# Gate rows by broadcast DMA, and the sample state laid out by sample, head and key quarter for VectorE, in a one-core decoder layer

## The chip, the core and the metric

The kernel runs on one core of a Trainium2 chip, as one program. The metric is the device time of one execution in microseconds. The core has a matrix engine (TensorE, PE in the rows), VectorE (DVE), ScalarE (ACT), GpSimd (POOL), and SyncE (SP), which here only issues DMAs. TensorE writes to PSUM; the other data live in SBUF (on chip, 128 partitions) and in DRAM.

## What is computed

One inference step of a decoder layer for a prompt of 1024 tokens and 8 single-token samples (1032 columns in all), model width 1024, everything float32. Cut to what matters here:

```
p = x @ w_in                      # pool input u | q | k | v | o | i gate, f gate (4 heads of 128)
y_pool = causal means over 2/4/8/16 tokens, minus token, per-group 128x128 map
b = cumsum(log f); m_t = running max; Dw = exp(b_t - b_s + i_s - m_t), causal
iw = exp(b + m_prev - m_t)        # weight of the carried state
s = (q k^T) * Dw
h = (s v + iw * q C) / max(|s 1 + iw * q n|, exp(-m_t))
C_new = g * C + sum_s w_s k_s v_s^T ;  n_new = g * n + sum_s w_s k_s
x1 = LN(alpha*x + [y_pool, sigmoid(o)*h] @ w_out);  x2 = LN(alpha*x1 + relu(x1 w1 + b1)^2 w2 + b2)
```

The prompt starts from a zero state. Each of the 8 samples has a state C of its own for each of the 4 heads: 32 matrices of 128 keys by 128 values, 2 MB, that are read (iw * q C), updated (one k v^T each) and returned.

## The kernel before

Activations lie transposed: channels on partitions, the 1032 tokens in the free dimension, in three blocks of 344 columns (BLK). Each float32 operand of a large product is split into a high part and a rounding rest (`x_hi`, `x_lo`, `w_hi`, `w_lo`), and a product is three float32r matmuls for each of the 8 slices of the inner dimension: 24 matmuls of 344 columns, called one product below. The order on each engine is written out by hand; counting semaphores tie the engines together.

**Projection.** Units u = 1 to 10 hold 256 weight columns each and give six products (i = 0 to 5). ScalarE evacuates each (`evac`), ScalarE and VectorE split the next weights (`split_hi`, `split_lo`). A product's bank is one of three, so it waits for the evacuation of the product three before it. Units 9 and 10 give the pool channels; VectorE forms their moving sums in `window(g, ..)`, twice a unit, after i = 3 and i = 5.

**Attention in the gaps.** The prompt is handled in 16 pairs p (4 heads, each 4 pairs of 128-token chunks). From unit 3 on one part of a pair stands behind each product (`gap_pair`): `att1`, `att2`, `att3`, so units 9 and 10 hold pairs 12, 13 and 14, 15. In att1 TensorE transposes the last pair's `h_nat`, spreads two gate rows of the head (the exponent row and iw) over 128 partitions by four matmuls of 256 columns with a 0/1 matrix (`select` by `rows_hi`, `rows_lo`), forms q k^T and transposes k and v. ScalarE (`decay_and_v`) turns the spread row into `decay` and copies v; GpSimd masks it; VectorE forms `q_inter` (q times the spread iw), `k_weighted`, `probs`, and gates the last pair's h. att2 is the state sum on TensorE and its addition to `state_ring` on VectorE, att3 numerator and denominator. att2 waits for `k_weighted`, att3 for the first `state_ring` update.

**Samples.** `sample_C` holds keys on partitions. GpSimd loads it in four DMAs after head 2. In att3 of pairs 12 to 15 TensorE multiplies one head's eight matrices with one column of q each (8 matmuls of one column). The update is in the output product.

**Output product.** Units 11 to 22: for each block four units of two products. After each product of the first block from the second on, TensorE makes an outer product of 512 columns (`outer`), four states at a time, from k (`kv_sample_nat`) and v masked by VectorE (`v_masked`, `vmask`); VectorE adds it to four matrices (`new_C`). The eighth stands behind the first product of unit 15. Then come the transposes of the mixed rows (`mix_T`), which wait for all of `C_new` in the case of the first tile, and the first layer norm (`ln1_a`). GpSimd stores the state (`C_s`) and only then loads `x_nat`, which `ln1_a` needs. The feed-forward part behind it is not touched.

## Time and profile before

| | us |
|---|---|
| median of 3 runs | 1136.58 |
| lowest, highest | 1135.8, 1137.31 |
| the profiled execution | 1137.68 |
| its span in the trace | 1134.8 |
| TensorE busy in the span | 1097.5 |

Start times below are microseconds from the start of the span. Between start times of neighbours in a TensorE timeline lies the true pace; a matmul's own length there contains its pipeline and overlaps the next. Lines L1666 and L1670 are the helpers for a matmul and a transpose, so groups are told apart by the names of the tiles (output<-inputs). A float32 matmul has two records.

### The profile page before, as it was taken

What the parts mean: (1) busy time and instruction counts of PE and PEld (TensorE: products, weight loads), DVE (VectorE), ACT (ScalarE), POOL (GpSimd) and SP (SyncE); (2) the same over time, 40 slices, a digit from 0 to 9 for tenths busy, and PEclk for the clock granted to TensorE, in tenths of its full rate; (3) what the DMA queues carried; (4) which work ended last, traced back from release to release, by engine and by line L of the source; (5) the groups of instructions that cost most, each with busy time, mean ns of one, the idle gap of its engine ahead of it and who ended that gap; (6) DMA issues with size and microseconds to landing.
All of it is one profiled execution on the core that took longest, in us unless ns stands there. A gap on an engine that the chain in (4) does not pass through costs nothing. (4 is left out here: it accounts for less than half of the span.)

```text
span 1134.8 us, 19572 instructions
## 1 busy us (share of the span) xinstructions
PE 1097.5 (97%) x8192; PEld 1078.6 (95%) x8192; DVE 663.8 (58%) x926; ACT 489.5 (43%) x694; POOL 90.3 (8%) x110
## 2 busy tenths in 40 slices
PE   7999999999999999999999999999999999999993
PEld 5999999999978899999999999999999999999993
DVE  5522222224567566495555655557766677878876
ACT  5622424241254366665554554545453323334022
POOL 4000000010010122000000000000000000000056
PEclk9999999999999999999999999999999999999997
DMA  9211111122115553124436354468734425334212
GB/s 252 75 47 33 40 39 39 41 84 62 38 45 164 185 175 106 51 66 156 151 121 184 113 151 147 131 183 271 271 103 141 146 80 168 115 114 165 75 49 101
DMA packets 93073, 132.70 MB, mean 117 GB/s; under 512 B 5369, under 2 KB 54105, under 8 KB 92996
## 3 DMA queue, kind: packets, MB, share of 16 engines
q1 hardware_dynamic: 89452, 121.13, 33.7%
q0 software_dynamic: 3552, 10.59, 3.2%
q8 instruction: 51, 0.84, 0.3%
q14 instruction: 18, 0.15, 0.0%
HBM read 97.04 MB, written 34.89 MB: 116 GB/s over the span
## 5 line engine op out<-in xcount | busy, mean ns | idle before, releaser
L1666 PE MATMUL bank<-x_hi,w_hi 128*128 128x344 f32 (+1 forms) x792 | 261.7, 330 | 3.0 <-DVE x_lo L1231 1.4
L1666 PE MATMUL bank<-x_hi,w_lo 128*128 128x344 f32 (+1 forms) x792 | 254.4, 321 | 0.0
L1666 PE MATMUL bank<-x_lo,w_hi 128*128 128x344 f32 (+1 forms) x792 | 254.1, 321 | 0.0
L1666 PE MATMUL bank<-x_hi,d_lo 128*128 128x258 f32 x1000 | 231.3, 282 | 0.0
L1666 PEld LDWEIGHTS bank<-x_hi,d_lo 128*128 128x128 f32 x1000 | 171.7, 189 | 0.0
L1666 PEld LDWEIGHTS bank<-x_hi,w_hi 128*128 128x128 f32 (+1 forms) x792 | 148.4, 187 | 10.8 <-issue 3.8
L1666 PEld LDWEIGHTS bank<-x_hi,w_lo 128*128 128x128 f32 (+1 forms) x792 | 148.1, 187 | 1.3
L1666 PEld LDWEIGHTS bank<-x_lo,w_hi 128*128 128x128 f32 (+1 forms) x792 | 148.2, 187 | 1.1
L1666 PE MATMUL bank<-x_hi,s_hi 128*128 128x258 f32 x448 | 126.5, 282 | 1.8 <-DVE s_raw_lo L1359 1.8
L1666 PE MATMUL bank<-x_lo,s_hi 128*128 128x258 f32 x448 | 126.5, 282 | 0.0
L1666 PE MATMUL bank<-t_hi,s_hi 128*128 128x258 f32 x336 | 95.2, 283 | 0.0
L1666 PE MATMUL bank<-t_lo,s_hi 128*128 128x258 f32 x336 | 95.1, 283 | 0.0
L1666 PEld LDWEIGHTS bank<-x_hi,s_hi 128*128 128x128 f32 x448 | 84.7, 189 | 2.0 <-DVE s_raw_lo L1359 2.0
L1666 PEld LDWEIGHTS bank<-x_lo,s_hi 128*128 128x128 f32 x448 | 84.5, 189 | 0.0
L1666 PE MATMUL bank<-x_hi 128*128 128x258 f32 x288 | 81.6, 283 | 0.0
L1666 PE MATMUL bank<-x_hi,x_lo 128*128 128x258 f32 x280 | 79.3, 283 | 2.3 <-DVE y_acc L1493 2.3
L1666 PE MATMUL bank<-x_lo,x_hi 128*128 128x258 f32 x288 | 81.4, 283 | 0.0
L1012 DVE TENSOR_TENSOR w_lo<-w_raw,w_hi 128x2048 fp32r<-128x2048 f32 x23 | 53.0, 2302 | 46.3 <-ACT w_hi L646 45.8
L903 ACT ACTIVATE x_hi<-x_lo_raw 128x2064 fp32r<-128x2064 f32 (+1 forms) x28 | 48.0, 1714 | 73.5 <-DMA x_lo_raw<-h_ops 73.5
L1666 PE MATMUL bank<-x_lo,d_lo 128*128 128x258 f32 x248 | 70.0, 282 | 0.0
L1666 PE MATMUL bank<-x_lo 128*128 128x258 f32 x248 | 69.9, 282 | 0.0
L1666 PEld LDWEIGHTS bank<-t_lo,s_hi 128*128 128x128 f32 x336 | 63.7, 189 | 0.0
(311 smaller groups left out, 2262.6 us busy)
## 6 DMA issues: line engine op xcount, KB each, us to landing
h_ops<-h_unit SPq DMA_DIRECT2D x56, 258.0 KB, 2.5
x_lo_raw<-h_ops SPq DMA_DIRECT2D x14, 1032.0 KB, 5.2
s_raw<-in_w_ff SPq DMA_DIRECT2D x14, 1024.0 KB, 7.0
w_raw<-in_w_out SPq DMA_DIRECT2D x12, 1024.0 KB, 5.1
x_lo_raw<-h_ops SPq DMA_DIRECT2D x14, 774.0 KB, 4.6
d_raw<-in_w_ff SPq DMA_DIRECT2D x9, 1024.0 KB, 7.4
w_raw<-in_w_in SPq DMA_DIRECT2D x16, 512.0 KB, 5.3
h_ops<-t_out SPq DMA_DIRECT2D x28, 258.0 KB, 5.1
```

The lines of the kernel that those rows point to most:

```text
L903: A(h_slot(t, XH), h_slot(t, XLS), ACT.Copy).then_inc(dh_hi, 1)
L1012: V.tensor_tensor(WL[:, q, :], RAW[:, q, :], WH[:, q, :].bitcast(F32), ALU.subtract).then_inc(lo_done, 1)
L1666: return nc.tensor.matmul(out, lhsT, rhs, start=start, stop=stop, skip_group_check=True)
```

## The change

**Gate rows.** The `select` matmuls, their high and low rows and their preparation on GpSimd, VectorE and ScalarE are gone. GpSimd writes the two rows of all heads to DRAM in two DMAs; SyncE reads them back in eight steps of two DMAs (`load_rows`), each giving 128 partitions the same 512 tokens (256 KB) of one head, in a ring of three; `decay` and `q_inter` read the ring in SBUF.

**Samples.** `sample_C` now has sample and head (32) times key quarter (4) on the partitions and 32 keys by 128 values in each. q, k and v of the samples are transposed in unit 9, sent to DRAM and back in nine DMAs in that layout. VectorE multiplies and adds eight keys at a time (`q_times_C`, four calls in unit 10); one small matmul adds the quarters. The update is two calls of `new_C` on VectorE alone, at the second and third unit of the output product; `outer` and `vmask` are gone. The C store stands behind the first `x_nat` loads. Core of the diff:

```diff
+        rows_d = nc.dram_tensor("gate_rows_d", (2, NH, SEQ), F32, kind="Internal").ap()
+
+        def row_slice(p, g):
+            return BR[:, p // 2 % 3, g, 2 * P * (p % 2):2 * P * (p % 2 + 1)]
...
+            def load_rows(d):
+
+                h, t0 = d // 2, 4 * P * (d % 2)
+                if d == 0:
+                    sp.wait_ge(rows_out, 32)
+                elif d >= 3:
+                    sp.wait_ge(E_ready, 4 * (d - 2))
+                    sp.wait_ge(qi_ready, 2 * (d - 2))
+                for g in range(2):
+                    sp.dma_start(BR[:, d % 3, g, :], rows_d[g, h:h + 1, t0:t0 + 4 * P].to_broadcast([P, 4 * P])).then_inc(bc_in[d % 3], 16)
...
+                if u >= 4:
+                    load_rows(u - 4)
...
+                if u == U_OUT:
+                    load_rows(7)
...
+            pool.wait_ge(dve_row, ROW_NEGM)
+            pool.dma_start(rows_d[0, :, :], TN[0:NH, pr]).then_inc(rows_out, 16)
+            pool.wait_ge(act_row, 4)
+            pool.dma_start(rows_d[1, :, :], RC[32:32 + NH, pr]).then_inc(rows_out, 16)
...
+                    if h == NH - 1 and j == 0:
+                        pool.wait_ge(kvs_read, 1)
+                        pool.dma_start(sn_d.rearrange("c r d -> r c d"), SN[0:32, :, :]).then_inc(sn_out, 16)
+                    elif h == NH - 1 and j == 1:
+                        pool.wait_ge(sn_out, 16)
+                        for q in range(4):
+                            pool.dma_start(QKS[32 * q:32 * (q + 1), :, :],
+                                           sn_d[0:2, :, 32 * q:32 * (q + 1)].rearrange("c r x -> r c x")).then_inc(qk_in, 16)
+                        for q in range(4):
+                            pool.dma_start(VS[32 * q:32 * (q + 1), :], sn_d[2]).then_inc(vs_in, 16)
...
-                    for s in range(NH):
-                        pool.dma_start(C0[:, s, :, :], a["state_C"][0, :, s, :, :].rearrange("b d e -> d b e"))\
-                            .then_inc(c_in, 16)
+                    for q in range(4):
+                        pool.dma_start(C0[32 * q:32 * (q + 1), :, :], state_v(a["state_C"], q)).then_inc(c_in, 16)
...
+                if t == 0:
+                    store_C(0)
+                    store_C(1)
...
+                    if UCH[u, f] == 0 and b == 0:
+                        act.wait_ge(qC_ready, 4)
                     A(Y[:, UCH[u, f], blk(b)], src, ACT.Copy).then_inc(gemm_read, 1)
...
-                act.wait_ge(bc_ready, p + 1)
+                act.wait_ge(bc_in[p // 2 % 3], 32 * (p // 6 + 1))
                 if p:
                     act.wait_ge(P_ready, p)
                 for i in range(2):
-                    A(E[:, i, :], B_[:, P * i:P * (i + 1)], ACT.Exp,
+                    A(E[:, i, :], row_slice(p, 0)[:, P * i:P * (i + 1)], ACT.Exp,
...
+                    if u == 9 and i == 2:
+                        act.wait_ge(kvs_T, 1)
+                        A(SN[0:32, :, :], B_[0:32, 0:384].rearrange("p (i n) -> p i n", i=3), ACT.Copy).then_inc(kvs_read, 1)
...
-            dve.wait_ge(act_row, 8)
-            V.tensor_tensor(RBL[0:NH, pr], TN[0:NH, pr], RBH[0:NH, pr].bitcast(F32), ALU.subtract)
-            row(V.tensor_tensor(RBL[32:32 + NH, :], RC[32:32 + NH, :], RBH[32:32 + NH, :].bitcast(F32),
-                                ALU.subtract), ROW_LO)
...
-                V.tensor_tensor(QI[:, :, :].rearrange("p i n -> p (i n)"), QKV[h % 2][:, 0, cs], B_[:, 256:512],
+                V.tensor_tensor(QI[:, :, :].rearrange("p i n -> p (i n)"), QKV[h % 2][:, 0, cs], row_slice(p, 1),
...
+                if p == NPAIR - 1:
+                    V.tensor_copy(ST[:, 7, :, :], N_[:, 264:296].rearrange("p (b h) -> p h b", h=NH))
...
+            def q_times_C(x):
+
+                dve.wait_ge(c_in, 64)
+                dve.wait_ge(qk_in, 64)
+                if x:
+                    dve.wait_ge(qC_ready, x)
+                step(V.tensor_tensor(PRODQ[:, :, :], C0[:, 8 * x:8 * (x + 1), :], of_planes(0, 8 * x, 8), ALU.mult))
+                for n in (4, 2):
+                    step(V.tensor_tensor(PRODQ[:, 0:n, :], PRODQ[:, 0:n, :], PRODQ[:, n:2 * n, :], ALU.add))
+                if x:
+                    step(V.tensor_tensor(PRODQ[:, 0, :], PRODQ[:, 0, :], PRODQ[:, 1, :], ALU.add))
+                    V.tensor_tensor(RP[:, :], RP[:, :], PRODQ[:, 0, :], ALU.add).then_inc(qC_ready, 1)
+                else:
+                    V.tensor_tensor(RP[:, :], PRODQ[:, 0, :], PRODQ[:, 1, :], ALU.add).then_inc(qC_ready, 1)
...
+                if u == 6:
+                    step(V.tensor_reduce(ROWSEL[:, :, :].rearrange("p b h -> p (b h)"),
+                                         IDN[:, :].rearrange("p (q r) -> p r q", q=4), AX.X, ALU.add))
+                    step(V.tensor_tensor(ST[:, 9, :, :].rearrange("p h b -> p (h b)").rearrange("p (b h) -> p b h", h=NH),
+                                         ROWSEL[:, :, :], iw_s.rearrange("p h b -> p b h"), ALU.mult))
+                    step(V.tensor_reduce(IW[:, 0:1], ST[:, 9:10, :, :].rearrange("p o h b -> p o (h b)"), AX.X, ALU.add))
...
+                    if u == 10 and i < 3:
+                        q_times_C(i)
+                        if i == 2:
+                            q_times_C(3)
...
+            def new_C(x):
+
+                dve.wait_ge(vs_in, 64)
+                if x:
+                    dve.wait_ge(C_new, x)
+                planes = C0[:, 16 * x:16 * (x + 1), :]
+                step(V.tensor_tensor(PROD[:, :, :], VS[:, :].rearrange("p (o e) -> p o e", o=1).to_broadcast([P, 16, DH]),
+                                     of_planes(1, 16 * x, 16), ALU.mult))
+                stt(planes, planes, IW[:, 0:1], PROD[:, :, :], ALU.mult, ALU.add).then_inc(C_new, 1)
+
...
                 b, j = (u - U_OUT) // 4, (u - U_OUT) % 4
-                if u == U_OUT:
-                    vmask(0)
                 if b == 0:
-                    vmask(2 * j + 1)
-                    new_C(2 * j)
                     split_lo(u + 2)
-                    if j < 3:
-                        vmask(2 * j + 2)
-                    new_C(2 * j + 1)
                     cat_lo_part(1 + j // 2, j % 2 == 0)
+                    if j in (1, 2):
+                        new_C(j - 1)
                 else:
...
-                    pe.wait_ge(qi_ready, p)
                     pe.wait_ge(kw_ready, p)
...
-                for g in range(2):
-                    mm(B_[:, 256 * g:256 * (g + 1)], SEL[:, g, h, :], RBH[:, cs], True, False)
-                    last = mm(B_[:, 256 * g:256 * (g + 1)], SEL[:, g, h, :], RBL[:, cs], False, True)
-                last.then_inc(bc_ready, 1)
...
-                if p >= NPAIR - NH:
-
-                    s = p - (NPAIR - NH)
-                    if s == 0:
-                        pe.wait_ge(c_in, 16 * NH)
-                        pe.wait_ge(prod_ready, 1)
-                        mm(N_[:, 300:364], ONES[:, :], ST[:, 0:2, :, :].rearrange("p a h b -> p (a h b)"))
-                    for b in range(NS):
-                        last = mm(N_[:, 264 + b:265 + b], C0[:, s, b, :], ST[:, 2, s, b:b + 1])
+                if p == NPAIR - NH:
+                    pe.wait_ge(prod_ready, 1)
+                    last = mm(N_[:, 300:364], ONES[:, :], ST[:, 0:2, :, :].rearrange("p a h b -> p (a h b)"))
+                elif p == NPAIR - 1:
+                    pe.wait_ge(qC_ready, 4)
+                    last = mm(N_[:, 264:296], RP[:, :], ROWSEL[:, :, :].rearrange("p b h -> p (b h)"))
...
+                    if u == 9 and i == 1:
+                        pe.wait_ge(smp_n, 1)
+                        for x, rows in enumerate((ST[:, 2, :, :], SM[:, 1, :, :], ST[:, 8, :, :])):
+                            last = tr(B_[0:32, P * x:P * (x + 1)], rows.rearrange("p x y -> p (x y)"))
+                        last.then_inc(kvs_T, 1)
...
-                    pe.wait_ge(C_new, 32)
+                    pe.wait_ge(nat_read, 2)
...
-                        else:
-                            pe.wait_ge(nat_read, 1)
-                            outer(2 * j + f - 1)
...
-                        if b == 1 and j == f == 0:
-                            outer(7)
```

TensorE, att1 of pair 14, before (`h_nat` is the last pair's output, `qkv_56` the q, k, v of the head):

```order
L1670 MATMUL bank<-identity,h_nat 128x128 x2
L1666 MATMUL bank<-rows_hi,select 128x256
L1666 MATMUL bank<-rows_lo,select 128x256
L1666 MATMUL bank<-rows_hi,select 128x256
L1666 MATMUL bank<-rows_lo,select 128x256
L1666 MATMUL bank<-qkv_56 128x128 x2
L1670 MATMUL bank<-identity,qkv_56 128x128 x4
L1666 MATMUL bank<-x_hi,w_hi 128x344
```

and now:

```order
L1724 MATMUL bank<-identity,h_nat 128x128 x2
L1720 MATMUL bank<-qkv_56 128x128 x2
L1724 MATMUL bank<-identity,qkv_56 128x128 x4
L1720 MATMUL bank<-x_hi,w_hi 128x344
L1720 MATMUL bank<-x_lo,w_hi 128x344
```

The four matmuls with `select` are gone; the transposes stand directly ahead of q k^T.

VectorE, unit 10, from pair 14's last att1 operation on, before (`state_ring` is att2's update, `small` att3's):

```order
L1106 TENSOR_TENSOR y_acc<-bank,y_acc 128x256
L1138 SCALAR_TENSOR_TENSOR state_ring<-state_ring,bc_cols,bank 128x129 x2
L1146 TENSOR_TENSOR small<-bank,gate_cols 128x2
L1148 SCALAR_TENSOR_TENSOR small<-bank,small 128x2
L1153 COPY sample_tmp<-bank 128x8
L1156 RECIPROCAL small<-small 128x2
L1113 TENSOR_TENSOR q_inter<-qkv_56,bank 128x256
```

and now (`state_prod_q` and `state_qC` belong to `q_times_C`):

```order
L1143 TENSOR_TENSOR y_acc<-bank,y_acc 128x256
L1245 TENSOR_TENSOR state_prod_q<-sample_C,state_qk 128x1024
L1247 TENSOR_TENSOR state_prod_q<-state_prod_q 128x512
L1247 TENSOR_TENSOR state_prod_q<-state_prod_q 128x256
L1252 TENSOR_TENSOR state_qC<-state_prod_q 128x128
L1175 SCALAR_TENSOR_TENSOR state_ring<-state_ring,bc_cols,bank 128x129 x2
L1245 TENSOR_TENSOR state_prod_q<-sample_C,state_qk 128x1024
L1247 TENSOR_TENSOR state_prod_q<-state_prod_q 128x512
L1247 TENSOR_TENSOR state_prod_q<-state_prod_q 128x256
L1249 TENSOR_TENSOR state_prod_q<-state_prod_q 128x128
L1250 TENSOR_TENSOR state_qC<-state_qC,state_prod_q 128x128
L1183 TENSOR_TENSOR small<-bank,gate_cols 128x2
```

Two further calls, ten rows, stand between att3 of pair 14 and `q_inter` of pair 15.

VectorE, output product, second unit of the first block, before:

```order
L1260 TENSOR_TENSOR v_masked<-kv_sample_nat,identity 32x512
L1269 SCALAR_TENSOR_TENSOR sample_C<-sample_C,bc_cols,bank 128x128 x4
L1012 TENSOR_TENSOR w_lo<-w_raw,w_hi 128x2048
L1260 TENSOR_TENSOR v_masked<-kv_sample_nat,identity 32x512
L1269 SCALAR_TENSOR_TENSOR sample_C<-sample_C,bc_cols,bank 128x128 x4
L1231 TENSOR_TENSOR x_lo<-y_acc,x_hi 128x4x344
```

and now (the last row begins the next unit):

```order
L1055 TENSOR_TENSOR w_lo<-w_raw,w_hi 128x2048
L1297 TENSOR_TENSOR x_lo<-y_acc,x_hi 128x4x344
L1324 TENSOR_TENSOR state_prod<-state_v,state_qk 128x2048
L1326 SCALAR_TENSOR_TENSOR sample_C<-sample_C,state_decay,state_prod 128x2048
L1055 TENSOR_TENSOR w_lo<-w_raw,w_hi 128x2048
```

The maskings and eight small updates of a unit have become one pair of 2048 columns, behind `x_lo`.

## Rows read from the trace of the kernel before

**Rows 1.** Page, part 1: busy time, share of span and instructions of TensorE.
```profile
PE 1097.5 (97%) x8192; PEld 1078.6 (95%) x8192; DVE 663.8 (58%) x926; ACT 489.5 (43%) x694; POOL 90.3 (8%) x110
```

**Rows 2.** TensorE timeline, att1 of pair 4: start, length, engine, instruction.
```profile
124.06 0.37 PE L1666 MATMUL bank<-rows_hi,select 128*128 128x256 f32 x1
...
124.62 0.61 PE L1666 MATMUL bank<-qkv 128*128 128x128 f32 x4
```

**Rows 3.** TensorE timeline, units 9 and 10, at pairs 13 and 14.
```profile
278.58 0.46 PE L1666 MATMUL bank<-v_aug,probs 128*128 128x129 f32 x2 [1.04 <-DVE state_ring L1138]
...
279.54 2.29 PE L1666 MATMUL bank<-sample_tmp,sample_C 128*128 128x1 f32 x16
281.70 0.63 PE L1666 MATMUL bank<-x_hi,w_hi 128*128 128x344 f32 x1
...
288.22 0.38 PE L1670 MATMUL bank<-identity,h_nat 128*128 128x128 f32 x2
...
289.71 0.41 PE L1666 MATMUL bank<-x_hi,w_hi 128*128 128x344 f32 x1
...
298.69 1.84 PE L1666 MATMUL bank<-sample_tmp,sample_C 128*128 128x1 f32 x16
300.40 0.40 PE L1666 MATMUL bank<-x_hi,w_hi 128*128 128x344 f32 x1
...
304.27 0.38 PE L1670 MATMUL bank<-identity,h_nat 128*128 128x128 f32 x2
...
316.44 1.98 PE L1666 MATMUL bank<-y_acc,w_pool_sb 128*128 128x344 f32 x6
```

**Rows 4.** Busy by window; the number before the last two is the granted clock.
```profile
282.00:284.00 2.00, 2.00 (x8) 2.00 (x8) 1.90 (x9) 1.47 (x3) 0.00 (x0) 0.50 0.00 0
372.00:376.00 4.00, 4.00 (x29) 4.00 (x28) 0.90 (x1) 0.00 (x0) 1.68 (x3) 1.00 0.98 267
```

**Rows 5.** TensorE timeline, output product, to the first mix transposes.
```profile
335.11 0.42 PE L1666 MATMUL bank<-x_hi,w_hi 128*128 128x344 f32 x1
...
340.11 0.42 PE L1666 MATMUL bank<-x_hi,w_hi 128*128 128x344 f32 x1
...
369.11 1.12 PE L1666 MATMUL bank<-v_masked,kv_sample_nat 32*128 32x512 f32 x2
371.54 0.63 PE L1670 MATMUL bank<-identity,y_acc 128*128 128x128 f32 x4 [1.31 <-DVE sample_C L1269]
...
386.30 0.42 PE L1666 MATMUL bank<-x_hi,w_hi 128*128 128x344 f32 x1 [0.62 <-DVE w_lo L1012]
```

**Rows 6.** VectorE timeline, end of unit 9 and unit 10.
```profile
281.87 0.16 DVE L1146 TENSOR_TENSOR small<-bank,gate_cols 128x2 f32<-128x2 f32 x1 [3.20 <-PE bank L1666]
...
288.08 2.28 DVE L1012 TENSOR_TENSOR w_lo<-w_raw,w_hi 128x2048 fp32r<-128x2048 f32 x1
290.28 0.41 DVE L1113 TENSOR_TENSOR q_inter<-qkv,bank 128x256 f32<-128x256 f32 x1
...
305.82 0.42 DVE L1113 TENSOR_TENSOR q_inter<-qkv,bank 128x256 f32<-128x256 f32 x1 [4.62 <-ACT decay L723]
306.46 0.42 DVE L1116 TENSOR_TENSOR k_weighted<-bank,gate_cols 128x256 f32<-128x256 f32 x1 [0.22 <-ACT v_aug L728]
...
311.87 0.73 DVE L1138 SCALAR_TENSOR_TENSOR state_ring<-state_ring,bc_cols,bank 128x129 f32<-128x129 f32 x2
```

**Rows 7.** ScalarE timeline, the evacuation ahead of pair 15's decay.
```profile
304.46 0.46 ACT L680 ACTIVATE y_acc<-bank 128x344 f32<-128x344 f32 x1 [2.60 <-PE bank L1666]
```

**Rows 8.** VectorE timeline, output product: `vmask`, then `x_lo` of a block.
```profile
338.66 0.67 DVE L1260 TENSOR_TENSOR v_masked<-kv_sample_nat,identity 32x512 f32<-32x512 f32 x1
...
341.26 1.59 DVE L1231 TENSOR_TENSOR x_lo<-y_acc,x_hi 128x1376 fp32r<-128x1376 f32 x1
```

**Rows 9.** DMA issues by line, size and time to landing: nearest broadcast load.
```profile
ln_gb<-in_ln_b POOLq DMA_DIRECT2D x1, 512.0 KB, 5.1
```

**Rows 10.** VectorE timeline, first residual of the first normalisation.
```profile
378.49 1.28 DVE L1299 SCALAR_TENSOR_TENSOR res_nat<-x_nat,bank 128x512 f32<-128x512 f32 x2 [5.59 <-DMA x_nat<-in_x_prompt]
```

More of the change, by code:

```diff
@@ L197, in build_layer @@
         pool_step, smp_kept, wsum_ready = sem("pool_step"), sem("smp_kept"), sem("wsum_ready")
-        bc_ready, s_ready, kvT_ready = sem("bc_ready"), sem("s_ready"), sem("kvT_ready")
+        s_ready, kvT_ready = sem("s_ready"), sem("kvT_ready")
+        rows_out, bc_in = sem("rows_out"), [sem(f"bc_in{x}") for x in range(3)]
         dC_ready, num_ready = sem("dC_ready"), sem("num_ready")
@@ L557, in _ @@
             G.memset(TN[0:NH, :], 1.0).then_inc(pool_step, 1)
-            pool.wait_ge(pool_step, 4)
+            pool.wait_ge(pool_step, 2)
             G.memset(TN[0:NH, pr].rearrange("h (c t) -> h c t", t=P)[:, :, 0:1], 0.0).then_inc(consts, 1)
@@ L603, in _, with store_C @@
             pool.dma_start(a["n_p"][0, 0, :, :], NN[32:36, :]).then_inc(nat_out, 16)
-            for h in range(NH):
-                pool.wait_ge(C_new, NS * (h + 1))
-                pool.dma_start(a["C_s"][0, :, h, :, :].rearrange("b d e -> d b e"), C0[:, h, :, :]).then_inc(c_out, 16)
+            def store_C(x):
+                pool.wait_ge(C_new, x + 1)
+                for q in range(4):
+                    pool.dma_start(state_v(a["C_s"], q)[:, 16 * x:16 * (x + 1), :],
+                                   C0[32 * q:32 * (q + 1), 16 * x:16 * (x + 1), :]).then_inc(c_out, 16)
             pool.wait_ge(nat_out, 16 * 7)
```

90 lines of the change are left out of this document (33 added, 57 removed).

## The prediction

> **What bounds the kernel now.** First the page's busy shares: TensorE is busy for 1097.5 us of a span of 1134.8, VectorE for little more than half [rows 1]. So an instruction taken off TensorE shortens the run by the time to the next start behind it, as long as VectorE and ScalarE deliver in time; work off the other engines brings nothing by itself. Then the TensorE timeline of the stretches that the change touches: the true cost of an inserted piece is the distance of start times, since lengths overlap. Last, the VectorE timeline of units 9 and 10, because there VectorE is already the last to arrive: TensorE stands 1.04 us ahead of pair 13's att3 until the first `state_ring` update, which queues behind a window sum [rows 3].
>
> A product with a following float32 step takes 3.87 us (300.40 to 304.27) [rows 3]; without the slower first matmul (0.40 long, the others about 0.32) 3.79. The att1 between two products takes 1.49 (288.22 to 289.71), and att2 and att3 together the rest of the 16.05 to the next att1 at 304.27, which holds three products and pair 14's sample matmuls: 1.24 [rows 3]. I call T the start of unit 10's first product, 281.70 in the trace.
>
> **Gate rows.** The four `select` matmuls take 0.56 us from their first start to that of q k^T (124.06 to 124.62) [rows 2]. There are 16 pairs: 14 stand ahead of T, which makes 7.8 us, and two behind. The operands of `decay` and `q_inter` now come by DMA. GpSimd's two writes are issued when the rows exist, before unit 3; SyncE's reads stand in its queue behind the weights of unit u and ahead of those of unit u + 1, and are issued about two units ahead of their use. A pair takes 16.05 us less the samples' 1.71, 14.3 us (288.22 to 304.27, 298.69 to 300.40) [rows 3], so two units are 57 us. The nearest row for such a load, 512 KB spread over 128 partitions, took 5.1 us to land [rows 9]; a step here moves as much. Cost zero, with 50 us of cover. The ScalarE and VectorE splits of the rows that fall away lie beside full TensorE work: zero.
>
> **Samples, ahead of T.** Eight one-column matmuls cost 1.71 us in pair 14 (298.69 to 300.40) and 2.16 in pair 13 (279.54 to 281.70) [rows 3]. Pair 12 I take as 1.7. Three transposes of 32 columns are added, two of them moved here from the output product; I take 0.1 us each, 0.3. Ahead of T: 7.8 + 1.7 + 2.2 - 0.3 = 11.4 us. Pair 13's wait stays: both sides of it move up by the same 0.56 us.
>
> **Unit 10.** Before, T to the first pool map is 34.74 us (281.70 to 316.44) [rows 3]. In it TensorE ran at half clock: the granted clock was 0.50 at 282 to 284 [rows 4], and the first product took 6.52 us instead of 3.87 (281.70 to 288.22) [rows 3]. Ahead of the fall stood the idle 1.04 us and then the one-column matmuls. The half-clock loss is 2.65 us. TensorE's own work after the change: 34.74 - 2.65 - 2 x 1.71 - 2 x 0.56 + 0.2 for the new small matmul = 27.75 us. That is the floor.
>
> But VectorE gets four `q_times_C` in this unit, which stand ahead of what TensorE waits for. Their price, from the nearest rows: a multiplication of 1024 columns a little over half of the split's 2.28 for 2048 [rows 6], 1.22; a sum of 512 as the masking in 0.67 [rows 8], of 256 as `q_inter` in 0.41, of 128 between that and the 0.16 of a two-column one [rows 6], 0.3. With about 0.03 for each wait between dependent steps that is 2.7 for the first and 3.0 for the others, 11.7 in all. The ends: 10 us if the narrow sums cost 0.16, 16 if broadcast and in-place operands cost a third more. I take 11.7, since the masking row has broadcast operands too and is no slower than its width.
>
> VectorE from T: att3 of pair 13 and the window sum, 0.17 and 6.1 (281.87 to 288.08, less a copy); the weight split 2.2 (to 290.28); att1 of pair 14, 1.4 (four of 0.41, overlapping) [rows 6]: T + 9.9. Four calls, one state update of 0.8 and att3's small steps of 0.5: T + 22.9. Now ScalarE, which has waited for the last call because the products of `q_times_C` lie in the channel that it evacuates next, needs what the trace shows from that evacuation (304.46) [rows 7] to `k_weighted` (306.46) [rows 6], 2.0 us, less the 0.24 in which `decay` waited for the spread rows: `k_weighted` starts at T + 24.7 and ends at T + 25.1. From its start to the next state update are 5.41 us (306.46 to 311.87) [rows 6], with a window sum in it; its first half ends at T + 30.5.
>
> TensorE from T: product 3.87, att1 1.49 - 0.56, product, att2 0.35 (after a wait of 0.6 for pair 14's `k_weighted`), product, att3 0.89, product, att1, product: T + 23.1, where it waits 2.0 us for pair 15's `k_weighted`. Then att2 and a product to T + 29.3, and 1.2 us for the state update; att3 and the small matmul 1.1: T + 31.6. So unit 10 gives 34.7 - 31.6 = 3.1 us instead of the 7.0 that TensorE's work alone would give. The chain is VectorE's from T on; whether the first product still runs at half clock does not matter.
>
> **The start of the output product** hangs on the pool maps and their evacuation as before, at the same distance. The last window sum ends some 2 us ahead of its map. No change.
>
> **Output product.** With an outer product a product takes 5.00 us (335.11 to 340.11) [rows 5], without one 3.79: 1.21, seven times, 8.5 us. The eighth stands ahead of the first mix transposes with 1.31 us of waiting: 369.11 to 371.54, 2.4 us [rows 5]. Two transposes gone: 0.2. VectorE's first residual waits 5.59 us for `x_nat`, which GpSimd loads behind the state stores [rows 10]; with the loads first this goes, and with it, I expect, TensorE's 0.62 us for `w_lo` at 386.30 [rows 5]. Sum 11.7 us. The new update is two operations of 2048 columns twice, 2 x 2.28 each time [rows 6], in a unit of 7.6 us in which VectorE has also 2.28 for the split and 1.59 for `x_lo` [rows 8]: 8.5 us, 0.9 more than the unit, in two units in a row. The split of unit u + 2 ends some 1.6 us or more ahead of its use, so I take zero; without that cover it costs 1 to 2 us. GpSimd's eight store DMAs now stand ahead of its first normalisation; they are issued by the time VectorE has its numbers.
>
> **Sum.** 11.4 + 3.1 + 11.7 = 26.2 us. From the profiled 1137.68 that gives 1111.5; this execution is 1.1 above the median of 1136.58, so the forecast is 1110.4.
>
> **The rivals.**
>
> A. VectorE keeps up: the calls are shorter, or ride in gaps. Then unit 10 falls to its floor, 3.9 us less: 1106.5. For it: the rows bound the narrow sums only loosely. Against: even at 10 us the chain is above the floor by 2. Chance 0.15.
>
> B. The clock. The new wait of 2.0 us and the one of 1.2 behind it could bring TensorE to 1.2 GHz again. In the trace 1.04 us of waiting followed by one-column matmuls was followed by the fall, while 1.31 us ahead of the mix transposes was not: the clock stood at 1.00 at 372 to 376 [rows 4, 5]. A product then costs 2.65 us more: 1113.1. Chance 0.18. The Trainium skill, "TensorE: Matmul & The Clock Gate", section "HAM oscillation — how this bites in real kernels", says that waits between bursts of matmuls let the clock fall and that each fall is paid anew; by it, the time would be the 1113.1 of this rival. The 1.31 us here, without a fall, does not bear that out for short waits.
>
> C. VectorE is slower than its rows, 16 us for the calls: 4.3 us later at the end of unit 10, 1114.7. Chance 0.12.
>
> D. Slower than before: the spread rows come late. ScalarE's `decay` in unit d + 3 waits for the load issued at the start of unit d + 1, and pair by pair TensorE behind it. Each of eight loads may take 57 us; what it takes beyond is paid in full, and 26.2 us are eaten at 60.3 us a load. At 61 us the time would be 1110.4 + 8 x 4 = 1142.4. The landing of 5.1 us [rows 9] and queues that idle between weight loads speak against it. Chance 0.03.
>
> **How the numbers follow.** Forecast 0.52 (1108 to 1112), A 0.15, B 0.18, C 0.12, D 0.03. The range takes in A, B and C with a microsecond beyond A's and C's ends for the terms outside unit 10: 1105.5 to 1116. About 0.2% (2.3 us) is what a measurement can tell from no change; faster by more than that 0.95, within it 0.02, slower 0.03.
>
> **What would show it.** No `select` row, and 0.93 us from `h_nat` to the next product instead of 1.49. In unit 10 a TensorE wait of about 2 us ahead of the last att2, released by `k_weighted`, and about 1 us ahead of the last att3, released by `state_ring`. Products 3.8 us apart in the first block of the output product, no wait of VectorE for `x_nat`. I am wrong if `decay` waits for a DMA, if the calls take over 4 us or under 2.4, if PEclk falls in unit 10, or if `w_lo` is late in units 13 to 16.

## The result: 20 us faster, 6 us less than forecast

| | before | after |
|---|---|---|
| median, us | 1136.19 (4 runs) | 1116.25 (4 runs, 1114.24 to 1116.7) |
| the profiled execution | 1137.68 | 1116.19 |
| its span | 1134.8 | 1114.4 |

The ratio is 0.9828, 95% interval 0.9816 to 0.984. The forecast was 1110.4 with a range of 1105.5 to 1116.0: the direction was right, the size was not, and the median lies 0.25 us above the range. Five more runs of the changed kernel beside new runs of the one before gave 1116.46 and 0.9832 (0.9818 to 0.9845).

The first thing to read is by how much the changed kernel is ahead at places that both kernels have. Each time is the start of a row in the TensorE timelines of the two profiled executions.

| place | before | after | ahead by | gained since the last | forecast |
|---|---|---|---|---|---|
| first matmul of the gates | 15.61 | 17.70 | -2.09 | -2.1 | 0 |
| first product of unit 1 | 31.38 | 34.09 | -2.71 | -0.6 | 0 |
| T, first product of unit 10 | 281.70 | 274.11 | 7.59 | 10.3 | 11.4 |
| first pool map | 316.44 | 306.03 | 10.41 | 2.8 | 3.1 |
| first product held by x_lo of the feed-forward part | 475.57 | 452.91 | 22.66 | 12.25 | 11.7 |
| first matmul of the down projection held by y_acc | 800.94 | 779.28 | 21.66 | -1.0 | 0 |
| the next one held by y_acc | 1061.86 | 1041.68 | 20.18 | -1.5 | 0 |
| span | 1134.8 | 1114.4 | 20.4 | 0.2 | 0 |

So the three stretches that the forecast worked out gave 25.4 of its 26.2 us. The other 5 went in two places to which it had given no thought: the first 34 us, and a wait about 400 us behind the last edited instruction. (The profiled times differ by 21.5 us and not by 20.4, since 1.1 us less lies outside the span in after; and the profiled execution of before is 1.5 above the median of the later runs, which is why the medians differ by 19.9.)

The page of after, part 1 (busy time, share of the span, instructions), answers to [rows 1]. TensorE's busy time fell by 24.7 us, the span by 20.4: some of what was taken off it became waiting.

```profile
PE 1072.8 (96%) x8051; PEld 1060.7 (95%) x8051; DVE 667.9 (60%) x905; ACT 486.8 (44%) x692; POOL 97.1 (9%) x122
```

**Unit 10.** The TensorE timeline of after, answering to [rows 3] (start, length, engine, instruction, in brackets the wait ahead of it and what ended it):

```profile
273.22 0.46 PE L1720 MATMUL bank<-v_aug,probs 128*128 128x129 f32 x2 [0.99 <-DVE state_ring L1175]
...
274.11 0.41 PE L1720 MATMUL bank<-x_hi,w_hi 128*128 128x344 f32 x1
...
277.97 0.38 PE L1724 MATMUL bank<-identity,h_nat 128*128 128x128 f32 x2
278.18 0.61 PE L1720 MATMUL bank<-qkv 128*128 128x128 f32 x4
...
278.98 0.40 PE L1720 MATMUL bank<-x_hi,w_hi 128*128 128x344 f32 x1
...
283.75 0.71 PE L1720 MATMUL bank<-v_aug,k_weighted 128*128 128x129 f32 x4 [0.74 <-DVE k_weighted L1153]
...
299.27 0.71 PE L1720 MATMUL bank<-v_aug,k_weighted 128*128 128x129 f32 x4 [1.47 <-DVE k_weighted L1153]
...
304.92 0.46 PE L1720 MATMUL bank<-v_aug,probs 128*128 128x129 f32 x2 [1.15 <-DVE state_ring L1175]
...
306.03 0.54 PE L1720 MATMUL bank<-y_acc,w_pool_sb 128*128 128x344 f32 x1
```

The reader sees the forecast chain: pair 13's wait is still there (0.99); att2 of pair 14 waits 0.74 (0.6 was forecast), the last att2 1.47 (2.0), the last att3 1.15 (1.2). T to the first pool map is 31.92 us; 31.6 was forecast. The first product behind T takes 3.86 us (274.11 to 277.97), where it took 6.52 at half clock before [rows 3, 4]. The att1 from `h_nat` to the next product takes 1.01 us (277.97 to 278.98), not the forecast 0.93.

VectorE's timeline of after in the same unit, the first call, the start of the second, the end of the fourth, and pair 15's first two operations, answers to [rows 6]:

```profile
284.28 1.21 DVE L1245 TENSOR_TENSOR state_prod_q<-sample_C,state_qk 128x1024 f32<-128x1024 f32 x1
...
286.71 0.29 DVE L1252 TENSOR_TENSOR state_qC<-state_prod_q 128x128 f32<-128x128 f32 x1
286.92 0.73 DVE L1175 SCALAR_TENSOR_TENSOR state_ring<-state_ring,bc_cols,bank 128x129 f32<-128x129 f32 x2
287.56 1.22 DVE L1245 TENSOR_TENSOR state_prod_q<-sample_C,state_qk 128x1024 f32<-128x1024 f32 x1
...
297.00 0.29 DVE L1250 TENSOR_TENSOR state_qC<-state_qC,state_prod_q 128x128 f32<-128x128 f32 x1
298.45 0.42 DVE L1150 TENSOR_TENSOR q_inter<-qkv,rows_bc 128x256 f32<-128x256 f32 x1 [1.16 <-ACT decay L765]
298.80 0.42 DVE L1153 TENSOR_TENSOR k_weighted<-bank,gate_cols 128x256 f32<-128x256 f32 x1
```

The first call takes 2.64 us (284.28 to 286.92), the second 2.98 (287.56 to 290.54). VectorE reached T + 10.17 with its first call; T + 9.9 was forecast. Its last call ends at T + 23.2, 0.3 later than forecast. `k_weighted` starts at T + 24.69; T + 24.7 was forecast. That this agrees to 0.01 us is luck: from ScalarE's evacuation behind the last call (297.39) to `k_weighted` (298.80) it is 1.41 us and not the 1.76 of the forecast, which made good the 0.3.

**Output product.** ScalarE's timeline of after (two evacuations in a row), then TensorE's first mix transposes, then VectorE's update of half of the state and its first residual:

```profile
323.59 0.46 ACT L828 ACTIVATE y_acc<-bank 128x344 f32<-128x344 f32 x1 [3.13 <-PE bank L1720]
...
327.36 0.46 ACT L828 ACTIVATE y_acc<-bank 128x344 f32<-128x344 f32 x1 [0.27 <-PE bank L1720]
```
```profile
349.75 1.03 PE L1724 MATMUL bank<-identity,y_acc 128*128 128x128 f32 x8
```
```profile
337.13 2.29 DVE L1324 TENSOR_TENSOR state_prod<-state_v,state_qk 128x2048 f32<-128x2048 f32 x1
339.45 2.35 DVE L1326 SCALAR_TENSOR_TENSOR sample_C<-sample_C,state_decay,state_prod 128x2048 f32<-128x2048 f32 x1
...
353.71 1.28 DVE L1358 SCALAR_TENSOR_TENSOR res_nat<-x_nat,bank 128x512 f32<-128x512 f32 x2
```

A product takes 3.77 us now (323.59 to 327.36) and took 5.00 [rows 5]. Neither the transposes nor the residual waits; 1.31 and 5.59 us of waiting are gone [rows 5, 10], and no `w_lo` is late.

**The start.** TensorE's timelines at the last x tile, before and after, each followed by GpSimd's two large constant loads of the same kernel. (These rows of before were not read for the prediction.)

```profile
14.47 1.42 PE L1670 MATMUL bank<-identity,x_nat_all 88*128 88x88 f32 x8 [1.54 <-DMA x_nat_all<-in_x_prompt]
15.61 0.57 PE L1666 MATMUL bank<-x_hi,w_hi 128*36 128x344 f32 x1
```
```profile
8.20 0.56 POOL L547 DMA_DIRECT2D state_pool_nat<-in_state_pool  x1
8.73 0.82 POOL L548 DMA_DIRECT2D w_pool_sb<-in_w_pool  x1
```
```profile
16.55 1.44 PE L1724 MATMUL bank<-identity,x_nat_all 88*128 88x88 f32 x8 [1.86 <-DMA x_nat_all<-in_x_prompt]
17.70 0.57 PE L1720 MATMUL bank<-x_hi,w_hi 128*36 128x344 f32 x1
```
```profile
5.13 0.55 POOL L572 DMA_DIRECT2D state_pool_nat<-in_state_pool  x1
5.67 0.81 POOL L573 DMA_DIRECT2D w_pool_sb<-in_w_pool  x1
```

With the `select` preparation gone from the head of GpSimd's program, its constant loads go out 3.07 us earlier, and the x tile on which the gates wait lands 2.08 us later. SyncE's queue issues the x tiles, GpSimd's the constants: 496 KB, of which TensorE first reads at 31 us in before, now fall among tiles that it waits for. The clock made it worse: windows of after, then of before (the number before the last two is the granted clock, of which 1.00 is 2.4 GHz and 0.50 is 1.2):

```profile
18.00:20.00 2.00, 2.00 (x8) 1.27 (x7) 0.98 (x2) 0.46 (x1) 0.00 (x0) 0.50 1.10 260
```
```profile
18.00:20.00 2.00, 2.00 (x14) 1.43 (x13) 0.00 (x0) 0.00 (x0) 0.00 (x0) 1.00 1.09 250
```

The gates of before began at half clock too, but from their first matmul to unit 1 it is 15.77 us there and 16.39 in after (17.70 to 34.09): 0.6 us more.

**The down projection.** The first matmul that waits for `y_acc`, before and then after, with the window behind it in after:

```profile
800.94 0.36 PE L1666 MATMUL bank<-x_hi,x_lo 128*128 128x258 f32 x1 [2.28 <-DVE y_acc L1493]
```
```profile
779.28 0.55 PE L1720 MATMUL bank<-x_hi,x_lo 128*128 128x258 f32 x1 [3.48 <-DVE y_acc L1547]
```
```profile
779.00:781.00 2.00, 1.72 (x8) 1.75 (x9) 2.00 (x2) 2.00 (x2) 0.00 (x0) 0.55 1.06 387
```

It waits 1.2 us longer, and then TensorE runs at half clock (0.55 in this window, 1.00 at the same place before), which costs 1.5 more. Nothing in this stage was changed.

The wait hangs on one load. SyncE's queue in before, after, and e7_rows (the kernel before with the gate rows alone, below): a weight load, the last stores of `h_ops` (a DRAM tensor for the hidden activations), and the load of `h_ops`, which waits until they have landed.

```profile
782.07 0.45 SPq L437 DMA_DIRECT2D d_raw<-in_w_ff  x1
...
783.18 0.43 SPq L412 DMA_DIRECT2D h_ops<-t_out  x1
790.55 0.92 SPq L443 DMA_DIRECT2D x_lo_raw<-h_ops  x2
```
```profile
759.21 1.22 SPq L469 DMA_DIRECT2D d_raw<-in_w_ff  x1
...
761.02 0.43 SPq L444 DMA_DIRECT2D h_ops<-t_out  x1
768.76 0.92 SPq L475 DMA_DIRECT2D x_lo_raw<-h_ops  x2
```
```profile
771.51 0.46 SPq L456 DMA_DIRECT2D d_raw<-in_w_ff  x1
...
772.63 0.43 SPq L431 DMA_DIRECT2D h_ops<-t_out  x1
781.43 0.92 SPq L462 DMA_DIRECT2D x_lo_raw<-h_ops  x2
```

Measured back from the end of TensorE's preceding matmuls (798.66, 775.80 and 788.15), the load is issued 8.11, 7.04 and 6.72 us ahead. In all sixteen profiled executions this lead and TensorE's wait add up to 10.3 to 10.6 us: each microsecond by which the load goes out later is one of waiting.

### The profile page after: what moved, and what is told of

Its sections match the earlier page's. It is cut to its first block and busy times, and to the rows that moved or that the text cites. A ratio compares the mean times of both kernels' runs of the same rounds, so it can differ in the third digit from the quotient of the medians.

```text
span 1114.4 us, 19275 instructions
## 1 busy us (share of the span) xinstructions
PE 1072.8 (96%) x8051; PEld 1060.7 (95%) x8051; DVE 667.9 (60%) x905; ACT 486.8 (44%) x692; POOL 97.1 (9%) x122
```

## The experiments

Each kernel ran five or more times beside the kernel before. A difference between a variant and the changed kernel is one of medians, with the changed kernel at 1116.46 in the first group. The intervals of the ratios are 1.0 to 2.3 us to either side, so such a difference is good to 1 or 2 us. A shorter time is one between places in a profiled execution: in after and e0_after, the one kernel that was profiled twice, stretches of this kind agreed to some 0.1 us where the clock did the same.

**The changed kernel again (e0_after).**

> The changed kernel again, unaltered. Theory S (the start is late because GpSimd's constant loads now go out 3.1 us earlier and share the DMA engines with the x tiles): the first gate matmul again near 17.7 us of the trace (15.6 in the kernel before), ratio to before 0.982 to 0.984. Rival N (the late start in the one profile was scatter of that execution): the first gate matmul falls back towards 15.6 and the profile's span is 2.7 us shorter. The wait ahead of the first matmul of the down projection (3.48 us after, 2.28 before) is also looked at: if it is scatter of the DMA, it differs here.

1116.46 us, the first gate matmul at 17.59, the wait at the down projection 3.52 us with half clock behind it. Both losses came back: neither is scatter of one execution.

**GpSimd's work put back (e1_prep).**

```diff
+            G.memset(sel, 0.0).then_inc(pool_step, 1)
+            G.affine_select(out=sel, in_=sel, ...).then_inc(pool_step, 1)
+            G.tensor_copy(sel, sel).then_inc(pool_step, 1)
             G.memset(VA[:, :, DH:DH + 1], 1.0).then_inc(consts, 1)
             ...
             pool.dma_start(CN[r:r + n, :], ...)
```

> The changed kernel with GpSimd's three 1024-column operations (3.1 us) put back ahead of its constant loads; their output is not used. Theory S: the constant loads go out at 4.9 us again, the first gate matmul starts near 15.6, unit 1 near 31.4, and the time falls by 2.7 us against the changed kernel, to about 1113.5. Rival N: no difference, 1116.2. Rival V (the late start comes from VectorE's removed memsets or something else at the start, not from the loads): the gate matmul stays at 17.7.

1111.5 us, ratio 0.9789 (0.9773 to 0.9805): 5.0 us less than the changed kernel, for three operations more. TensorE's timeline and the window at 16 us:

```profile
14.75 0.83 PE L1731 MATMUL bank<-identity,x_nat_all 88*128 88x88 f32 x8 [1.04 <-DMA x_nat_all<-in_x_prompt]
15.37 0.37 PE L1727 MATMUL bank<-x_hi,w_hi 128*36 128x344 f32 x1
```
```profile
16.00:18.00 2.00, 2.00 (x15) 1.40 (x14) 0.77 (x2) 0.13 (x1) 0.00 (x0) 1.00 1.06 317
```

The gates start 2.33 us earlier and run at 1.00, so that unit 1 starts at 30.08, 4.0 us ahead of after's 34.09. The theory named the cause rightly and was short by the clock: it had reckoned with that of the kernel before. The rivals (scatter; VectorE's removed memsets) are out. The clock's part is not the loads' alone. e7_rows, whose GpSimd does the same as that of the kernel before up to its constant loads, has full clock too and takes 14.69 us from the first gate matmul to unit 1, as e1_prep does with 14.71, where before takes 15.77.

**The same order put into the kernel before (e5_early).** Only the preparation moved behind the constant loads, which go out at 1.83 us there:

> The kernel before with nothing changed but GpSimd's select preparation, which stands behind its constant loads instead of ahead of them, so that these go out 3.1 us earlier. Theory S: the first gate matmul moves from 15.6 to about 17.7, unit 1 from 31.4 to 34.1, and the kernel is 2.7 us slower than before, ratio 1.0024. Rivals N and V: no difference, ratio 1.000.

1138.9 us, ratio 1.0029 (1.0017 to 1.0041).

```profile
17.84 0.57 PE L1666 MATMUL bank<-x_hi,w_hi 128*36 128x344 f32 x1
```

The gates start 2.23 us later than in the kernel before, unit 1 at 33.68 instead of 31.38. The order of loads is a cost of its own, in a kernel that has none of the change. (The clock column of this execution stands at 1.00 in the window 18 to 20 us, though a gate matmul lasts 0.49 us there, as at 0.50 in after, and 0.32 at full clock. In the first microseconds the length of the matmuls is the safer sign.)

**The two large constant loads late (e2_late).**

```diff
+            pool.wait_ge(x_in[5], 16)
             pool.dma_start(SPN[0:NS * NBUF, :], ...)
             pool.dma_start(WP[:, :, :], ...)
```

> The changed kernel with the two large constant loads (state_pool_nat 240 KB, w_pool_sb 256 KB) issued only when the sixth x tile has landed. Theory S: 496 KB less between the x tiles at some 250 GB/s are 2.0 us, so the first gate matmul starts 2 us before that of the changed kernel or earlier, 15.0 to 15.7, and the time is 2 to 3.5 us shorter than the changed kernel's, 1112.7 to 1114.2. Rival N: no difference. Rival L (the loads are then late for the two transposes ahead of unit 1 at 31 to 34 us): a wait for a DMA there, no gain.

1111.27 us, ratio 0.9788 (0.9773 to 0.9802), 5.2 us less than the changed kernel. The gates start at 14.82, no wait for a DMA stands between them and unit 1 (29.55), so rival L is out. The forecast 15.0 to 15.7 was a little too late; the rest of the gain is again clock, which was at half from about 11 to 14 us, beside the transposes, and not beside the gates.

The Trainium skill, "DMA: Bandwidth & Descriptors", section "Queues, rings and completion order", says that each DMA engine goes round between the queues for which it has work, a packet at a time. By that rule a load in another queue is served beside the x tiles however late it is wanted, and e1, e2 and e5 agree with it.

**The gate rows alone (e7_rows).** The kernel before with the rows by DMA, and with the three GpSimd operations kept:

> The kernel before with only the gate rows by DMA; GpSimd's three operations ahead of its constant loads are kept, the samples are untouched. Theory: each att1 is 0.48 us shorter (the trace of after has 1.01 us from the transposes of h_nat to the next product instead of 1.49), 16 pairs give 7.7 us, ratio 0.9932 or 1128.5. The prediction's own price of 0.56 would give 9.0 us, ratio 0.9921. Rival: the row loads or the added waits cost something, and less than 7 us are left.

1129.97 us, ratio 0.9944 (0.9929 to 0.9958): 6.0 us, less than either 7.7 or 9.0. From pair to pair, `h_nat` of att1 comes 0.47 us earlier each time (1.86 us ahead of before at pair 1, 7.10 at pair 12: 5.24 in eleven pairs, 0.476 each). That is the theory's price. In the profiled execution, 1.35 us faster than the median, the clock added to it, 1.1 us at the start and 1.1 at unit 10's first product. But at the down projection there is the longer wait, with half clock behind it, as in after:

```profile
791.69 0.36 PE L1680 MATMUL bank<-x_hi,x_lo 128*128 128x258 f32 x1 [3.54 <-DVE y_acc L1507]
```

So the samples' part of the change is not needed for a long wait there. But it is not shown that the gate rows make it in both kernels, for the load of `h_ops` is late in two ways. Here the last store is issued on time, 15.5 us ahead of the matmuls' end as in before, and 8.8 us pass until the load; in the four kernels without row loads it is 7.0 to 7.4. In the eleven profiled executions with the whole change or a variant of it the issue of the weight load ahead of the last stores lasts 1.2 to 1.8 us instead of 0.45, the last store is issued 0.7 to 1.3 us later for it, and the distance from it to the load is 6.7 to 7.9. Why that issue lasts longer is not known.

The row loads themselves cost the projection nothing: in after the 16 took 5.4 us to land in the median (5.1 was forecast), and no `decay` waited for one.

**Unit 10 without the calls (e3_nocalls).**

> The changed kernel with the multiplications of q and C in unit 10 left out: each of the four calls is one small operation (0.3 and three of 0.15 us), so the sample outputs are not those of the reference. The theory (unit 10 is VectorE's chain): the waits ahead of the last att2 and att3 go, T to the first pool map falls from 31.9 to the floor of 27.8 us, 1112.1. Rival W (the window sums alone hold the last state update): a wait of 1 us or more stays ahead of the last att3 and 1113.5 or more is measured.

1112.71 us, ratio 0.9793 (0.9781 to 0.9806). The last att2 and att3 no longer wait. T is at 274.56, the first pool map at

```profile
303.36 0.54 PE L1715 MATMUL bank<-y_acc,w_pool_sb 128*128 128x344 f32 x1
```

which makes 28.80 us; 27.8 was expected. So the calls cost 3.1 us in unit 10 (31.92 - 28.80). The floor of the prediction, 27.75, was about 1 us too low: 0.74 of it is the wait ahead of pair 14's att2, which stands here too, and which VectorE's window sum and weight split cause ahead of the first call; 0.16 is the price of the spread rows, taken too high twice. This kernel leaves out what the calls compute; the next one keeps it.

**Two calls later (e4_later).**

```diff
-                    if u == 10 and i < 3:
+                    if u == 10 and i < 2:
                         q_times_C(i)
-                        if i == 2:
-                            q_times_C(3)
...
             split_lo(U_OUT + 1)
+            q_times_C(2)
+            q_times_C(3)
```

`state_qC`'s matmul goes behind the fourth product of the output product, the samples' numerator behind it, and ScalarE's `wait_ge(qC_ready, 4)` is gone, since `state_prod_q` lies elsewhere.

> The changed kernel with two of the four q_times_C calls and the sample numerator moved behind the weight split of the first output-product unit, where VectorE idled 6.4 and 3.7 us in the trace; state_prod_q lies in a free slot of the ring of gate rows, so ScalarE's evacuation no longer waits for the calls. Theory: as without the calls, T to the first pool map 27.8 to 28.2 us, no loss later, 1112.2. Rival M (moved, not removed): the calls come back as a wait of TensorE for w_lo or x_lo in the output product, and at most 1 us is gained.

1113.23 us, ratio 0.9799 (0.9786 to 0.9811). TensorE's last att2, last att3 and first pool map, none with a wait:

```profile
297.36 0.60 PE L1727 MATMUL bank<-v_aug,k_weighted 128*128 128x129 f32 x4
...
301.58 0.38 PE L1727 MATMUL bank<-v_aug,probs 128*128 128x129 f32 x2
...
302.47 0.45 PE L1727 MATMUL bank<-y_acc,w_pool_sb 128*128 128x344 f32 x1
```

From T (273.83) that is 28.64 us, as low as without the calls. From the pool map to the next common place, the first `x_lo` wait of the feed-forward part, it is 147.03 us, and 146.88 in after: the moved calls (from 315.78 on) came back nowhere, and rival M is out. Of the 3.28 us, some were lost to the clock later in this execution: behind a wait of 1.75 us, which after has too and where its clock held, it fell:

```profile
466.60 0.39 PE L1727 MATMUL bank<-x_hi,s_hi 128*128 128x258 f32 x1 [1.75 <-DVE s_raw_lo L1420]
```
```profile
467.00:471.00 4.00, 4.00 (x23) 4.00 (x23) 3.15 (x3) 2.02 (x2) 0.00 (x0) 0.60 1.01 305
```

**Both together (e6_both).**

> The later calls and the late constant loads together. The two stretches lie apart, so the gains should add: 4.0 and 2 to 3.5 us off the changed kernel, 1108.7 to 1110.2. Rival: one gain is given back at a later wait (the first of the down projection, whose length hangs on DMA landings), 1111 or more.

1110.23 us, ratio 0.9765 (0.9752 to 0.9777): with h2_best below the fastest kernel of the study, 6.2 us below the changed one. The two gains of 5.2 and 3.2 add to 8.4 and gave 6.2, a difference hardly larger than the 1 to 2 us that such a sum is good to. In its profile unit 1 starts at 29.79 and the pool maps at 298.45, 7.58 us ahead of after, nearly the sum; then the clock falls behind the 1.75 us wait (462 to 467 us, as in e4_later), which takes 1.5. So something was given back, as the rival said, but not where it said: the wait at the down projection is 3.46 us, as in after.

**What lengthens the wait at the down projection: addresses or the queue? (g1_addr, g2_poolq, h1_bothq)** Two things of the change reach that far: two new DRAM tensors move `h_ops` by 80 KB (in e7_rows one of them, by 32 KB), and SyncE's queue, which loads and stores for the down projection, has 16 transfers more behind it.

> The changed kernel with its two new DRAM tensors declared behind h_first and h_ops, so that these lie at the addresses that they have in the kernel before. Every kernel run so far with the row loads waits 3.1 to 3.6 us ahead of the first matmul of the down projection that needs y_acc, with TensorE at half clock behind it; both without them wait 1.8 and 2.3 us and keep the clock. Theory Q (the shifted DRAM addresses of h_ops slow its stores and loads): the wait falls to about 2.3, the clock stays at 1.00, 2.5 us are gained, 1113.8. Rival P (the 16 row loads in SyncE's queue change how its later transfers fall): no difference, wait 3.1 to 3.6, 1116.3.

> The changed kernel with the 16 row loads issued by GpSimd instead of SyncE, so that SyncE's queue is that of the kernel before; the DRAM tensors stay where the changed kernel has them. Theory P: the wait ahead of the down projection's matmul falls to about 2.3 us and the clock stays, 1113.8. Theory Q: no difference, 1116.3. Rival G (GpSimd's issues delay its masking of decay): waits of TensorE ahead of att3 in units 4 to 8, slower than 1116.3.

1115.13 us (0.9833, 0.9813 to 0.9853) and 1115.84 us (0.9835, 0.9814 to 0.9856). The waits were 2.86 and 2.90 us, the clock fell behind both. Each seemed to give half of the wait; in time neither gave anything that can be told, for the kernel before was faster in this group too (1134.45), and the ratios are that of the changed kernel, 0.9832.

> The changed kernel with both edits together: new DRAM tensors declared last, and the row loads issued by GpSimd. Each alone left a wait of 2.9 us ahead of the down projection where the changed kernel has 3.5 and the kernel before 2.3. If both contribute (theories P and Q each half), the wait is 2.3 here and the clock stays at 1.00 behind it, 1113.5. If neither matters (rival R: something else that the kernels with row loads share), 2.9 to 3.5 again and 1115.5 to 1116.3.

1115.77 us (0.9822, 0.9806 to 0.9839), a wait of 2.76 us with half clock behind it. The two do not add up, so neither is shown to be a cause.

**Each of them in the kernel before (h3_pad, h4_loads).**

> The kernel before with an 80 KB DRAM tensor declared ahead of h_first and h_ops (one row of it is written once), so that their addresses are those of the changed kernel. Theory Q: the wait ahead of the down projection rises from 2.3 to 2.9 or 3.5 us and TensorE is at half clock behind it, 1137.5 to 1138.5. Otherwise the wait stays at 1.8 to 2.3, ratio 1.000.

> The kernel before with 16 loads of the same shape and size as the row loads (one row of 512 words to 128 partitions) in SyncE's queue at units 4 to 8, into a tile that is free then; nothing reads them. Theory P: the wait ahead of the down projection rises to 2.9 to 3.5 us, half clock behind it, 1137.5 to 1138.5. Otherwise it stays at 1.8 to 2.3 and the time at that of the kernel before. It shows too what the loads cost the projection itself: nothing by the prediction.

1135.45 us (1.0002, 0.9993 to 1.0011) and 1135.73 us (1.0001, 0.9992 to 1.001). The rows at the down projection, h3_pad and then h4_loads:

```profile
801.25 0.36 PE L1670 MATMUL bank<-x_hi,x_lo 128*128 128x258 f32 x1 [1.90 <-DVE y_acc L1497]
```
```profile
801.08 0.36 PE L1676 MATMUL bank<-x_hi,x_lo 128*128 128x258 f32 x1 [1.86 <-DVE y_acc L1503]
```

Neither lengthens the wait, nor the issue of the weight load (0.45 and 0.46 us). Theories P and Q are both out as sole causes. h4_loads shows too, by a clean comparison, that 16 broadcast loads of 256 KB cost the projection nothing.

**Everything together (h2_best).**

> Two of the four calls later, the two large constant loads late, DRAM tensors last, row loads by GpSimd. The sum of what each brought: 1110.2 with the first two, and 0 to 2.7 us more from the other two, 1107.5 to 1110.2. Rival: an added fall of the clock at a wait of 1 to 2 us gives it back, 1110 or more.

1110.38 us (0.9775, 0.976 to 0.979), like e6_both: the wait was 3.58 us again.

## Why the prediction fell short, step by step

**"The four `select` matmuls take 0.56 us from their first start to that of q k^T": the mis-sized term.** It was priced by the distance that they span [rows 2]. But with them gone the q k^T starts 0.21 us behind the `h_nat` transposes (277.97 to 278.18 in after), where the first `select` matmul had started 0.13 behind (288.22 [rows 3] to 288.35). TensorE's timeline of before:

```profile
288.35 0.37 PE L1666 MATMUL bank<-rows_hi,select 128*128 128x256 f32 x1
```

The att1 shrank from 1.49 to 1.01: 0.48. Over 14 pairs 6.65 us instead of 7.8, a shortfall of 1.2. The distance to take was that of the neighbours on both sides of the piece, less what they will then keep between them.

**The samples ahead of T, 3.6 us: right.** What is left of the gain there is 7.59 + 2.71 - 6.65 = 3.65.

**"The ScalarE and VectorE splits ... lie beside full TensorE work: zero", and no word on GpSimd's: the missing step.** The account of the change names the preparation on GpSimd as gone; the prediction did not ask what stands behind it in GpSimd's program, and so put the whole start at nothing. It is the constant loads, and they came 3.07 us forward into the one stretch of the kernel where TensorE waits for DMA. It cost 2.1 us in DMA and 0.6 in clock against the kernel before; e1_prep and e2_late show that 4.0 and 4.5 us can be had there up to unit 1, since the clock can also stay up. Without these 2.7 us the median would have lain inside the range. A step taken out moves every instruction behind it, and that can be a loss.

**Unit 10, 31.6 us: right, 31.92.** Its chain held place by place, and so did the price of the calls (four calls of 2.6 to 3.2 us; 11.7 forecast in all). The wait at the last att2 was 1.5 and not 2.0 us, pair 14's att2 0.74 and not 0.6. The floor behind it, 27.75, was too low by 0.9 to 1.0: a wait that the prediction had itself put into the chain was left out of the floor. The value of rival A was thus 3.1 to 3.3 and not 3.9 us.

**Rival B, the clock in unit 10: did not come.** The waits of 1.47 and 1.15 us were followed by no fall; the window 282 to 290 and those behind it stand at 1.00. But clock falls did take part elsewhere, at places where only the length or the time of a wait changed. The prediction's "whether the first product still runs at half clock does not matter" was not put to the test: in all eleven profiled executions without the one-column matmuls that product ran at full clock (3.86 or 3.87 us).

**Rivals C and D: did not come.** The calls took 11.9 us, not 16; no row load was late.

**Output product, 11.7 us: 12.25.** A product's outer product cost 1.23 us rather than 1.21, and from the first mix transposes to the feed-forward part 0.87 us came (371.54 to 475.57 before, 349.75 to 452.91 after), where 0.62 had been credited. The rest lies ahead of the transposes. The state updates of 4.6 us in two units in a row cost TensorE nothing.

**Everything behind the output product: "not touched", and 2.5 us lost.** 1.2 us is the longer wait and 1.5 the clock fall behind it; 0.2 had been gained on the way there. The failed step is that an untouched part takes an unchanged time. The wait is 2.76 to 3.58 us in all twelve profiled executions with the row loads, e7_rows among them, and 1.83 to 2.28 in the four without. It is longer because SyncE issues the load of `h_ops` later, by 1.07 us in after: 0.7 because its last store went out late behind a slow issue, 0.4 because the stores took longer to land. In e7_rows all of the 1.4 us is the landing. The DRAM addresses alone, and loads of the same shape in the same queue alone, were put into the kernel before and do nothing. What of the change slows that issue and those stores stays open. Not tried: the placement of the SBUF tiles behind the ring, and the changed instruction streams. That the two together with something else are needed isn't excluded either.

The sum of the misses: 2.7 (start) + 1.1 (ahead of T) + 0.3 (unit 10) - 0.55 (output product) + 2.5 (down projection) - 0.2 (end) is 5.8 us, the forecast 26.2 less the 20.4 that the span gave.

## What to carry to other kernels

Removing work from an idle engine is not free when DMA issues stand behind it in that engine's program: list them, and ask what else is on the DMA engines then. Read the first microseconds, where TensorE waits for input, as carefully as the stretch that was edited, and keep loads that are wanted late out of them. Price a removed piece by what its neighbours will have between them without it, and give the range a term for clock falls at waits of 1 to 4 us that merely shift. Where an untouched stage slows down, trace its wait back to the issue of the load that ends it: that showed here two different delays behind one symptom.

## What the runs showed of the hardware

**The clock fell at some waits of 1 to 3.6 us and not at others, and at the same wait of the same code in some executions only.** The wait of 1.75 us ahead of the first `s_hi` matmul was followed by half clock in e4_later, e6_both, h2_best, h3_pad, g2_poolq and e3_nocalls, and not in before, after, e0_after, e1_prep, e2_late, e5_early, e7_rows, g1_addr, h1_bothq or h4_loads. The 1.82 us one of the down projection was followed by it in fourteen of the sixteen executions, but not in g1_addr and g2_poolq, which took 51.43 us from there to the next wait where before and after took 52.97. The 3.10 us at the down projection in e3_nocalls passed without a fall. A fall cost 1.5 us there. The ten runs of the kernel before in the first group spread over 1134.02 to 1137.5, a little more than two such falls; that they are the cause of the spread wasn't shown run by run. The Trainium skill, "TensorE: Matmul & The Clock Gate", section "HAM oscillation — how this bites in real kernels", says that waits between bursts let the clock fall; the traces bear that out for some of these waits only.

**One place where it always fell.** Pair 13's att3 waits 0.99 to 1.08 us in all sixteen. In the five kernels with the samples' one-column matmuls behind it the first product of unit 10 took 5.40 to 6.62 us (granted clock 0.50 in before [rows 4]); in the eleven without them 3.86 or 3.87.

**VectorE reads one operand broadcast, and writes in place, at hardly any extra cost**: 1024 columns with a broadcast operand 1.21 to 1.23 us, as in the window sum; 2048 columns 2.29 with a broadcast operand and 2.35 in place, where the plain split takes 2.28 [rows 6].

**One row of 512 words loaded to 128 partitions landed in 5.4 us in the median of 16 (after), and 16 such loads beside full TensorE work cost nothing** (h4_loads, 5.0 us to land, ratio 1.0001).
